# Nine norm statistics as two rounded passes, their low parts by VectorE, and ten products moved to GpSimd, in a two-layer hybrid decoder trunk

## The reference

```
h = rms_norm(x, attn_norm)
proj = h @ w_in            # all heads' inputs in one projection
o_gla = gated linear attention, 4 heads, chunks of 64 tokens
q_d, k_d = rms_norm(heads(d_q)), rms_norm(heads(d_k))      # DSA: 4 heads of 64
o_dsa = attention over the top 128 keys that an indexer picks for each query
q_m = heads(rms_norm(m_cq) @ mla_w_uq)                     # MLA: 4 heads of 96
k_nope, v_m = split(heads(rms_norm(m_ckv) @ mla_w_ukv))
q_m = rms_norm(q_m, mla_q_norm);  k_m = rms_norm(concat(k_nope, k_rope), mla_k_norm)
rotary on the last 32 features of q_m and k_m, then causal softmax attention
x = x + concat(norms and gates of o_gla, o_dsa, o_mla) @ w_out
x = x + square(relu(rms_norm(x, mlp_norm) @ w_up)) @ w_down
```

## Time and profile before

| | us |
|---|---|
| median of three runs | 1255.13 (1254.95 to 1256.62) |
| the profiled execution | 1253.49 |
| its span, first to last instruction | 1251.7 |
| PE busy | 1236.5 (99%) |
| DVE busy | 777.6 (62%) |
| ACT busy | 528.5 (42%) |
| POOL busy | 216.7 (17%) |
| stretch 62 to 150 us: PE / DVE / ACT / POOL busy | 85.8 / 85.0 / 47.0 / 26.4 of 88 |

### The profile page before, as it was taken

The page is one execution under the profiler, slowest core; times in us unless marked ns, Lnnn a source line. Parts: engine busy times, 40 slices in busy tenths (PEclk is TensorE's granted clock), DMA queues, the critical chain, the costliest instruction groups (busy, mean ns, idle before and its releaser), DMA issues.

```text
span 1251.7 us, 17687 instructions
## 1 busy us (share of the span) xinstructions
PE 1236.5 (99%) x5956; PEld 973.0 (78%) x5956; DVE 777.6 (62%) x1234; ACT 528.5 (42%) x858; POOL 216.7 (17%) x140
## 2 busy tenths in 40 slices
PE   8999999999999999999999999999999999999998
PEld 7766776688888888888886667767888888888887
DVE  6699988644644554544757999785446445445444
ACT  5674438643323224224437643585442242232331
POOL 1132330020120110210522234200201102102002
PEclk9999999999999999999999999999999999999999
DMA  6212220023232223322322222201232232233223
GB/s 242 89 51 68 68 85 2 17 102 116 99 101 91 95 98 101 101 84 101 101 89 81 68 68 68 69 2 46 89 101 90 96 101 101 84 101 101 95 98 109
DMA packets 30720, 108.36 MB, mean 87 GB/s; under 512 B 3536, under 2 KB 3536, under 8 KB 30672
## 3 DMA queue, kind: packets, MB, share of 16 engines
q1 hardware_dynamic: 29520, 103.82, 24.9%
q0 software_dynamic: 432, 2.86, 0.6%
q10 hardware_dynamic: 720, 1.07, 0.3%
HBM read 105.64 MB, written 2.10 MB: 86 GB/s over the span
## 4 chain that ended last, share of the span: by engine, by line
PE 82%; DVE 11%; issue 4%; ACT 3%; DMA 1%; ACTq 0%; DVEq 0%
PE bank L898 19%; PE bank L897 19%; PE bank L899 19%; PE bank L517 4%; PE bank L518 4%; PE bank L519 4%; PE bank L540 2%; PE bank L538 2%; PE bank L539 2%; PE bank L779 1%; PE bank L791 1%; DVE sel L1401 1%; PE bank L806 1%; DVE sel L1354 1%; DVE m L1350 1%
## 5 line engine op out<-in xcount | busy, mean ns | idle before, releaser
L952 ACT ACTIVATE wh<-raw 128x1024 fp32r<-128x1024 f32 x191 | 201.7, 1056 | 377.9 <-PE bank L899 246.5
L1275 DVE TENSOR_TENSOR wl<-raw,wh 128x1024 fp32r<-128x1024 f32 x155 | 240.5, 1552 | 75.6 <-ACT wh L952 75.5
L897 PE MATMUL bank<-hh,wl 128*128 128x512 f32 x512 | 200.0, 391 | 0.0
L897 PE MATMUL bank<-xmh,wl 128*128 128x512 f32 x512 | 199.3, 389 | 0.0
L899 PE MATMUL bank<-hl,wh 128*128 128x512 f32 x512 | 199.2, 389 | 0.0
L899 PE MATMUL bank<-xml,wh 128*128 128x512 f32 x512 | 199.2, 389 | 0.0
L898 PE MATMUL bank<-xmh,wh 128*128 128x512 f32 x512 | 199.2, 389 | 0.0
L898 PE MATMUL bank<-hh,wh 128*128 128x512 f32 x512 | 199.2, 389 | 0.0
L482 POOL TENSOR_TENSOR x<-x,rsb 128x512 f32<-128x512 f32 x62 | 82.0, 1322 | 587.4 <-DVE rsb L1696 587.4
L1685 DVE TENSOR_TENSOR sqb<-tf 128x512 f32<-128x512 f32 x64 | 44.3, 692 | 181.6 <-ACT hh L1238 181.6
L517 PE MATMUL bank<-xgh,wl 128*128 128x512 f32 x368 | 151.0, 410 | 2.7 <-DVE xgl L1288 2.5
(11 more groups left out here) (218 smaller groups left out, 1669.2 us busy)
## 6 DMA issues: line engine op xcount, KB each, us to landing
raw<-in_stream SPq DMA_DIRECT2D x191, 512.0 KB, 3.3
out_y<-x SPq DMA_DIRECT2D x8, 256.0 KB, 3.5
x<-in_x ACTq DMA_DIRECT2D x4, 256.0 KB, 7.0
x<-in_x SPq DMA_DIRECT2D x4, 256.0 KB, 7.1
con<-in_consts POOLq DMA_DIRECT2D x1, 976.5 KB, 5.2
par<-in_params POOLq DMA_DIRECT2D x1, 916.0 KB, 5.5
par<-in_params POOLq DMA_DIRECT2D x1, 896.0 KB, 6.9
raw<-in_stream SPq DMA_DIRECT2D x2, 256.0 KB, 4.1
```

Source lines behind the costliest of these rows:

```text
L897: pe.matmul(B.t[s][:], wl[:, s, n_block(k)], src_h[:, k], start=(k == 0), stop=False)
L952: act.activation(wh[:, s], raw[:, s], ACT.Copy).then_inc(hi_ready.sem, 1)
L1275: vec.tensor_tensor(wl[:, s], raw[:, s], wh[:, s], ALU.subtract).then_inc(lo_ready.sem, 1)
```

## The change

Statistics. For nine of the norm statistics (`mqst0..3`, `dqst1`, `dkst0`, `dkst1`, `mkst0`, `mkst1`) ACT squares into `sqb` as before, then copies the square rounded into `sqh` (fp32r), linked behind it; DVE subtracts `sqh` from `sqb` into `sql` (`square_low`); PE multiplies rounded ones (`ones_r` or `blk_r`) by `sqh` and by `sql`, where it had one f32 product. PE waits for `nsl_ready`, which DVE gives, where it waited for `nsq_ready` of ACT. `dqst0`, `cqst`, `ckvst` and the product with `turn_rows` stay f32.

Products on POOL. Ten products per layer go from DVE to POOL: `rb` times the decays (`scale_decay`, four; the constant 1/8 goes into DVE's read of `gq`), `cos` times the rotary rows of the queries (`turn_query`, four), and the keys to the end of a chunk (`key_end`, two). They stand between POOL's low parts.

Selection. Two steps go to slot 7, slots 12 to 15 get three instead of two, slots 19 to 22 get fewer. It stays at 48 steps per layer, 16 for each block of queries.

```diff
+SELECT = [3, 3] + [3, 2, 1] * (TOPK // 8 - 2) + [2, 1] * 2
...
+                def scale_decay(buf, pr):
+                    pool.wait_ge(*exp_ready.at(l, 1))
+                    src, dst = (e1, kinv) if buf == 0 else (e2, e2)
+                    pool.tensor_tensor(dst[:, pr], src[:, pr], rb[:], ALU.mult).then_inc(scaled.sem, 1)
+
+                def turn_query(h, ahead):
+                    pool.wait_ge(*ahead)
+                    pool.wait_ge(*q_copied.at(l, h))
+                    pool.tensor_tensor(tf[64:QK, h % 2], tf[64:QK, h % 2], cos, ALU.mult).then_inc(q_turned.sem, 1)
+                    pool.wait_ge(*q_turned.at(l, h))
...
                 for u in POOL_LOW:
                     pool.wait_ge(*hi_ready.at(l, u + AHEAD))
                     pool.tensor_tensor(wl[:, u % 2], raw[:, u % 2], wh[:, u % 2], ALU.subtract)\
                         .then_inc(lo_ready.sem, 1)
+                    if u == 9:
+                        pool.wait_ge(const_loaded, 16)
+                        scale_decay(0, 0)
+                        scale_decay(0, 1)
+                        turn_query(0, scaled.at(l, 1))
+                    if u in (10, 11):
+                        scale_decay(1, u - 10)
+                        turn_query(u - 9, scaled.at(l, u - 8))
+                    if u == 12:
+                        turn_query(3, lo_ready.at(l, u + AHEAD))
+                    if u in (14, 15):
+                        key_end(u - 14)
...
+            def stat_parts(l, name, lhsT, rows=P):
+                i = norm_index(name)
+                pe.wait_ge(*nsl_ready.at(l, i - FIRST_PART))
+                pe.wait_ge(*B.vacant(l, name))
+                pe.matmul(B[name][0:rows, :], lhsT, sqh[0:rows, i % 2], start=True, stop=False)
+                return pe.matmul(B[name][0:rows, :], lhsT, sql[0:rows, i % 2], start=False, stop=True)
...
                 unit(10)
                 mla_q_stat(0)
-                stat(l, "dqst1", blk, sq_of("dqst1"))
+                stat_parts(l, "dqst1", blk_r[:]).then_inc(*B.on_fill("dqst1"))
                 mla_q(1)
...
+                def square_high(name, src, rows=slice(0, P), wait=None):
+                    i = norm_index(name)
+                    if wait is not None:
+                        act.wait_ge(*wait)
+                    link(act.activation(sqb[rows, i % 2], src, ACT.Square))
+                    act.activation(sqh[rows, i % 2], sqb[rows, i % 2], ACT.Copy).then_inc(nsq_ready.sem, 1)
...
+                def square_low(name, rows=slice(0, P)):
+                    i = norm_index(name)
+                    vec.wait_ge(*nsq_ready.at(l, i))
+                    vec.tensor_tensor(sql[rows, i % 2], sqb[rows, i % 2], sqh[rows, i % 2], ALU.subtract)\
+                        .then_inc(nsl_ready.sem, 1)
...
                     vec.wait_ge(*q_copied.at(l, h))
-                    vec.tensor_tensor(tf[64:QK, h % 2], tf[64:QK, h % 2], cos, ALU.mult)
...
                     vec.wait_ge(*B.freed(l, f"mq{h}"))
+                    vec.wait_ge(*q_turned.at(l, h))
...
                     if u == 7:
+                        select_steps(0, 1)
                         weighted(3)
+                        select_steps(1, 1)
...
                     if u == 9:
                         mla_turn(0)
+                        square_low("mqst0", slice(0, QK))
                         dsa_queries(0)
+                        square_low("dqst1")
                     if u == 10:
                         mla_queries(0)
                         mla_turn(1)
+                        square_low("mqst1", slice(0, QK))
                         dsa_queries(1)
+                        square_low("dkst0")
...
                           *krb_ready.at(l, 0))
+                        square_low("mkst0")
                     if u in (14, 15):
                         pr = u - 14
...
+                        if pr == 0:
+                            square_low("mkst1")
                         mla_keys(pr)
...
-                per_slot = {9: 3, 10: 3, 11: 3, 12: 2, 13: 2, 14: 2, 15: 2, 16: 4, 17: 4, 18: 4,
-                            19: 5, 20: 5, 21: 5, 22: 4}
-                done = 0
+                per_slot = {9: 3, 10: 3, 11: 3, 12: 3, 13: 3, 14: 3, 15: 3, 16: 4, 17: 4, 18: 4,
+                            19: 4, 20: 4, 21: 3, 22: 2}
+                done = 2
```

More of the change, by code:

```diff
@@ L274, in build_trunk @@
         ones, _ = place("ones", [P, P])
+        ones_r, _ = place("ones_r", [P, P], F32R)
+        blk_r, _ = place("blk_r", [P, P], F32R)
         low_rows, _ = place("low_rows", [P, P])
@@ L353, in build_trunk @@
         q_copied = S("q_copied", H)
+        q_turned = S("q_turned", H)
+        scaled = S("scaled", 4)
         krb_ready = S("krb_ready")
@@ L592, in mla_q_stat @@
                 def mla_q_stat(h):
[L593 removed]
+                    pe.wait_ge(*blk_ready.at(0, 0))
+                    stat_parts(l, f"mqst{h}", ones_r[0:QK, 0:QK], QK).then_inc(*B.on_fill(f"mqst{h}"))
                 def mla_k(pr):
@@ L691, in _ @@
                 mla_q_stat(1)
-                stat(l, "dkst0", blk, sq_of("dkst0"))
+                stat_parts(l, "dkst0", blk_r[:]).then_inc(*B.on_fill("dkst0"))
                 mla_q(2)
@@ L695, in _ @@
                 mla_q_stat(2)
-                stat(l, "dkst1", blk, sq_of("dkst1"))
+                stat_parts(l, "dkst1", blk_r[:]).then_inc(*B.on_fill("dkst1"))
                 mla_q(3)
@@ L991, in _ @@
             act.wait_ge(const_loaded, 16)
+            act.activation(blk_r[:], blk, ACT.Copy).then_inc(blk_ready.sem, 1)
             for l in range(DEPTH):
@@ L1103, in tasks @@
                         factor("dqst0", DH)
-                        square("dqst1", dqr[:, 1], wait=B.freed(l, "dq1"))
+                        square_high("dqst1", dqr[:, 1], wait=B.freed(l, "dq1"))
                     if u == 10:
@@ L1108, in tasks @@
                         factor("dqst1", DH)
-                        square("dkst0", dkn[:, 0], wait=B.freed(l, "dk0"))
+                        square_high("dkst0", dkn[:, 0], wait=B.freed(l, "dk0"))
                     if u == 11:
@@ L1113, in tasks @@
                         factor("dkst0", DH)
-                        square("dkst1", dkn[:, 1], wait=B.freed(l, "dk1"))
+                        square_high("dkst1", dkn[:, 1], wait=B.freed(l, "dk1"))
                     if u == 12:
@@ L1120, in tasks @@
                         factor("mqst3", QK, QK)
-                        square("mkst0", B["mk0"][:], wait=B.filled(l, "mk0"))
+                        square_high("mkst0", B["mk0"][:], wait=B.filled(l, "mk0"))
                     if u == 14:
-                        square("mkst1", B["mk1"][:], wait=B.filled(l, "mk1"))
+                        square_high("mkst1", B["mk1"][:], wait=B.filled(l, "mk1"))
                     if u in (14, 15):
@@ L1270, in _ @@
             vec.memset(turn_rows[QK:P], 0.0).then_inc(rows_ready.sem, 1)
+            vec.memset(ones_r[:].bitcast(F32), 1.0).then_inc(rows_ready.sem, 1)
             def low_part(s, hi_wait):
@@ L1340, in select_steps @@
                 def select_steps(first, n):
-                    for i0 in range(first, first + n, 3):
-                        queries = [3 - i % 3 for i in range(i0, min(i0 + 3, first + n))]
+                    rest = SELECT[first:first + n]
+                    while rest:
+                        queries = rest[:3] if len(set(rest[:3])) == len(rest[:3]) else rest[:1]
+                        rest = rest[len(queries):]
                         found = {}
@@ L1501, in tasks @@
                         mla_turn(2)
+                        square_low("mqst2", slice(0, QK))
                         dsa_keys(0)
+                        square_low("dkst1")
                     if u == 12:
@@ L1505, in tasks @@
                         mla_turn(3)
+                        square_low("mqst3", slice(0, QK))
                         dsa_keys(1)
```

48 lines of the change are left out of this document (27 added, 21 removed).

## The result

The changed kernel takes 1262.45 us, the median of five executions (1262.10 to 1263.28), against 1256.54 (1254.95 to 1256.86) for the kernel before, measured beside it: ratio 1.0052 with an interval of 1.0037 to 1.0066. It is slower by some 6 us where 7 were forecast. The profiled execution has a span of 1260.7 us; that of before has 1251.7. These two differ by 9.0 and not by 6, because the executions of before scatter with their mean granted clock: over all that were listed with one, those at 1.000 take 1252.9 to 1253.2 us, those at 0.999 take 1253.3 to 1254.9, those at 0.998 take 1254.7 to 1255.3, those at 0.997 take 1256.2 to 1257.1, and the profiled one (1253.5, at 0.999) was among the fast. The forecast added 7.0 to the shown median of 1255.1. On the profiled execution's own base it gave 1260.5, and 1262.45 came.

What follows compares the result with a forecast made beforehand. PE was taken to set the time, DVE following about 4.5 us late. Per layer -3.6 +6.2 +0.9 +0.9 +0.5 -2.2 = +2.7, with 0.8 for the clock +3.5; +7.0 for both on 1255.1 gives 1262 us, range 1252.5 to 1267.

Steps and rivals of the forecast that it cites:

- What PE saves: Nine statistics per layer: two rounded products replace one f32 statistic, 0.40 us saved each, 3.6 us per layer.
- The stall in slot 10: Between units 10 and 11, PE waits for DVE's subtractions for mqst0 and dqst1: idle 6.2 us per layer.
- Slots 11 to 13: PE idle 0.9, 0.9 and 0.5 us there; turn_query on POOL costs DVE 0.95 through the lock.
- The value product's wait: In front of mv1, PE's wait of 2.2 us per layer goes and nothing is late in its place.
- The clock: In slot 10's waits PE's clock may fall: 0.8 us per layer taken, between nothing and 2 us.
- (a): Slot 10: lock misses new POOL products; stall 4.9 instead of 6.2 us; 1253 us, 1255 with clock lost; chance 0.17.
- (b): At the rounded statistics nobody waits, DVE being early enough; saving and lost wait give 11.6 us, 1243.5; chance 0.08.
- (c): Slots 10 and 11: POOL's low part before last subtraction; about 2.2 us each, 1270 us, one per layer 1266; chance 0.13.

Runs made afterwards that it cites:

- fillers: Changed kernel plus 17 and 4 rounded products per layer in front of the waits for mqst0 and dqst1, later overwritten: 1258.34 us, ratio 1.0035.
- the late selection: Changed kernel with 0, 1 and 2 selection steps instead of 3 each in slots 9 to 11, the rest moved to slots 17 to 21: 1246.16 us, ratio 0.9936.
- the late selection with the subtractions ahead: Against the late selection: one more step from slot 12 to 22, subtractions for dqst1, dkst0, dkst1 ahead of the DSA products: 1243.14 us, ratio 0.9901.

## Why the prediction was right, and where it was off

**What PE saves.** Two rounded products take 0.46 us (98.44 to 98.90) and 0.40 is saved, as stated. Behind a wait the pair takes about 0.57 (108.37 to 108.94, where the next product begins), a tenth more, which the sum didn't have; that is five times in a layer.

**The stall in slot 10.** This was the main term and it was met in each of its steps:

| step | forecast | measured |
|---|---|---|
| slot 9 begins | 0.9 late, 78.7 | 78.86 |
| DVE's subtraction for `mqst0` done | 85.4 | about 85.5 |
| PE starts `mqst0` | 85.5 | 85.70 |
| PE starts `dqst1` | 87.9 | 87.94 |
| unit 11 begins | 90.0 | 90.3 with fillers (90.50 less one product of 0.23); 92.4 in the changed kernel (92.80 less 0.42) |
| idle | 6.2 | 6.2 with fillers counted as idle (87.97 - 81.26 - 0.54, the last being the pair at 85.68) |

It was met because each step was laid out as turns on a lock, from rows that showed such turns. The Trainium skill (SBUF — State Buffer, "SBUF: two separate sides") calls the shared ports an exclusive lock for the whole instruction; the 2.27 us of a subtraction that takes 0.68 alone agree with that again. The ten products aren't the origin of the stall: in the kernel that has none of them on GpSimd the first wait was 4.2 as well. The lock does lengthen it, by some 1.6 us through the low part of the weights (2.27 less 0.68); the rest is that DVE comes to this subtraction late.

**Slots 11 to 13.** Waits of 0.9, 0.9 and 0.5 were forecast. With the clock kept up there came none in slot 11 and 0.40, 0.54 and 0.49 behind it, 1.4 together and 1.7 with the three slower pairs. In the timeline of DVE with fillers, slot 10 takes 8.0 us (87.95 to 95.95), and slot 11 takes 9.7. In the first POOL had only its rotary product. It came 4.5 us after the slot's start and not 4.2, behind DVE's add and beside the product that follows it (92.35), so it was POOL that waited (1.56 us instead of 1.08), and DVE lost nothing. In the second it had two products in a row (below, POOL of the same kernel):

```profile
99.63 1.70 DVE L1455 TENSOR_TENSOR tf<-tf,qT 32x512 f32<-32x512 f32 x1
101.37 1.46 DVE L1457 TENSOR_TENSOR qT<-tf,rsb 96x512 f32<-96x512 f32 x1
```

```profile
99.49 1.30 POOL L477 TENSOR_TENSOR e<-e,rb 128x512 f32<-128x512 f32 x1
100.87 1.42 POOL L482 TENSOR_TENSOR tf<-tf,con 32x512 f32<-32x512 f32 x1
```

DVE's add (99.63) ends behind POOL's first one, its product (101.37) behind the second: 1.8 us more than the 0.68 and 0.69 that the two take alone, where I had counted only `turn_query` and 0.95. So the lock costs 0 and 1.8 in the two slots instead of 0.95 twice; the sum is the same by luck. The step that failed is that `scale_decay(1, 1)`, which stands ahead of `turn_query(2)` in POOL's queue, was left out of slot 11.

**The value product's wait** went, as said, and nothing became late in its place. A small misreading on which nothing hangs: the second run of nines in DVE's line of the page begins in the 23rd slice, near 690 us, and not at 620.

**The clock** is the term that was mis-sized. I took 0.8 us per layer between bounds of 0 and 2; 2.05 was measured (4.1 in both layers, 2.72 in the first, so above the bound there, and 1.4 in the second). The second wait was also named too long, 2.4 instead of the 1.9 that the times of slot 10 give (87.9 less 85.5 less 0.46). The upper bound was taken from the start, 16 products that lose 2 us. In the stall of layer 0 all of PE's work from 85.70 to 93.65 ran at the half rate. What PE did in that time, two statistics of 0.46, `mq1` of 1.72 and three products of 0.23, is 3.3 us at the full rate; 3.3 more were lost, and 0.6 of them lay in the wait between the statistics, which shrank from 1.75 (fillers and wait) to 1.10. My reason for a low value, that DVE is late anyhow and hides part of the loss, was wrong beyond that: from 107.15 on PE waits for DVE as long as in the kernel with fillers (0.41 and 0.54 against 0.40 and 0.54), because DVE itself was held by PE's slow products. It waited 1.91 us in front of L1442 at 94.91 for ScalarE's copy out of `mq1`. The clock loss was handed on to DVE instead of being absorbed. The Trainium skill (TensorE: Matmul & The Clock Gate, "HAM oscillation — how this bites in real kernels") warns that waits between bursts bring the array back to the low rate and advises an order of work that leaves no such waits; here the low rate costs 4.1 us by the run with fillers, and the late selection, with a mean clock of 1.000, shows the better way of following it.

**The sum.** Without the clock 2.34 (layer 0) to 2.6 us per layer came, where I had 2.7: slots 11 to 13 were cheaper by 0.9 and the slower pairs dearer by 0.5, which gives the 2.3 of layer 0. The projection stage of layer 1 adds the same 2.34 (118.94 us against 116.60 from its first `cqn` product to the first with `ptb`), and 0.2 more arises in layer 0 between the first product with `ptb` and the first of the MLP (89.26 us with fillers, 89.04 in before); together 4.9, near the 5.1 of the medians. With the clock it is 4.6 by before at a full clock (1262.45 - 1253.2, halved), where I had 3.5. That the median came out within half a microsecond is owed to a second thing that I had not seen: the median of before, 1255.1, lies some 2 us above before at a full clock, most likely a clock loss of its own in the wait that the change removes. By luck the two mistakes have opposite signs.

**The rivals.** That the lock misses the products (a) was refuted by the rows at 77.42 and 85.53, where `scale_decay` holds DVE. That the statistics wait for nobody (b) is false for the change, and its number, 1243.5, is about what the late selection with the subtractions ahead then reached (1243.14). The collision of the low part with the last subtraction (c) didn't happen in slots 10 and 11: `dkst0`'s subtraction takes its usual 0.68 at 96.97 and POOL's low part follows at 99.85.

## What to carry to other kernels

A statistic moved onto a second engine saves passes only if that engine is on time at that place: look not at its busy share but at how far it runs behind, and put what can be done later (here the selection) behind what the other engine now waits for, before any work is moved elsewhere. A saving of 3.6 us per layer, with 2.2 of a wait that went, became a loss of 4.6, for the most part by two subtractions for which PE waited 4.2 and 1.1 us and by the clock that fell there; it became a gain of 1.0% once seven selection steps and three subtractions stood elsewhere. Two remedies for the same lateness need not add, as here, so try the one that costs nothing first.

## What the runs showed of the hardware that was not expected

- A wait of 2.2 us on TensorE seems to lower the granted clock in some executions and not in others: the same kernel takes 1252.9 to 1257.1 us at mean clocks of 1.000 to 0.997, and filling that wait took away the group at 1256, while the four kernels with late selection, whose waits in these slots are 0.5 us at most, stay within 0.06%. A scatter in steps is a hint to look for one wait of that length.
- The same waits, 4.22 us and 1.10 behind it, kept TensorE's work at 1.2 GHz for 8.0 us in layer 0 (85.70 to 93.65, though it worked without a gap from 88 us on) and for 5.3 in layer 1 of the same execution, at a price of 2.7 and 1.4 us. Behind 4.16 us of waiting in the kernel with the statistics alone the first statistic still ran at the full rate. One such stall thus has no single price.
- Behind a short wait two rounded products take 0.57 us and not 0.46, at a full clock.
- A product of two f32 tensors of 128x512 takes GpSimd 1.29 us in most cases (the shortest and the median of the 62 products `x<-x,rsb` of the changed kernel) and 1.07 in the four of `key_end`; the rotary one of 32x512 takes 1.08 (94.58). So the rotary product was forecast at 0.2 us too much, and a quarter of the partitions saves little. Why `key_end` is shorter at the same size isn't shown.
